# A two-layer transformer kernel: the experts' weight requests reordered, constant matmuls put into five waits, and the mLSTM heads begun right after the copy of their gates

## What is computed

```python
proj = rms_norm(x, norm_mix_g) @ w_in           # dq dk dv | mq mk mv mo | gates
y_da = rms_norm(diff_attention(dq, dk, dv), g)   # 4 heads x 128 columns
y_ml = sigmoid(mo) * normalise(mlstm(mq, mk, mv, gates))
x = x + concat(y_da, y_ml) @ w_out
x = x + cross_attention(rms_norm(x), mem)
# experts: top 2 of 32 for each token, h the normalised rows of an expert
x = x + sum_e weight_e * ((silu(h @ w1[e]) * (h @ w3[e])) @ w2[e])
x4 = rms_norm(rms_norm(x, norm_final_g), ln_a)
b, c, u, z = split(x4 @ w_in_a, 4)              # second block begins
```

## Time and profile before

| | us |
|---|---|
| median of 3 runs | 1514.36 (1511.99 to 1514.66) |
| the profiled execution | 1516.11 |
| its span, first to last instruction | 1514.3 |
| TensorE busy | 1339.1 (88%) |
| VectorE, ScalarE, GpSimd busy | 537.7, 414.4, 392.1 |
| mean granted TensorE clock | 0.946 |

### The profile page before, as it was taken

How to read it: one execution, slowest core, us unless ns; L and a number is a source line. 1 busy time by engine, 2 the same in 40 slices (tenths; PEclk the granted TensorE clock), 3 DMA queues, 4 the chain that set the end, 5 groups by cost and what they waited for, 6 DMA issues and landing times. The chain is left out here.

```text
span 1514.3 us, 16638 instructions
## 1 busy us (share of the span) xinstructions
PE 1339.1 (88%) x6268; PEld 887.8 (59%) x6268; DVE 537.7 (36%) x1074; ACT 414.4 (27%) x809; POOL 392.1 (26%) x372
## 2 busy tenths in 40 slices
PE   7999998999989679988887887883999999999799
PEld 6776775798758533323222222232888887788467
DVE  3649747421052421111111111117241414554753
ACT  5333365154231100000000000005322123444641
POOL 7553233168320112111111111100243550000331
PEclk9999997999999679999999999996999999999999
DMA  7221221144303849999999999994223231232000
GB/s 206 88 81 56 66 102 45 67 167 139 111 5 144 345 190 406 420 423 421 423 422 423 423 422 423 422 381 164 84 84 108 87 104 65 94 100 84 29 22 35
DMA packets 72368, 298.27 MB, mean 197 GB/s; under 512 B 10168, under 2 KB 10216, under 8 KB 51568
## 3 DMA queue, kind: packets, MB, share of 16 engines
q1 hardware_dynamic: 64848, 282.80, 47.6%
q0 software_dynamic: 7456, 14.59, 3.0%
HBM read 293.16 MB, written 12.58 MB: 202 GB/s over the span
## 5 line engine op out<-in xcount | busy, mean ns | idle before, releaser
L740 POOL TENSOR_TENSOR ring_rounded<-ring,ring_rounded 128x512 fp32r<-128x512 f32 x192 | 254.2, 1361 | 328.0 <-ACT ring_rounded L1435 328.0
L862 PE MATMUL bank<-HT_rounded,ring_rounded 128*128 128x512 f32 (+1 forms) x576 | 222.1, 386 | 5.9 <-DVE ring_rounded L2301 4.5
L864 PE MATMUL bank<-HT_rounded,ring_rounded 128*128 128x512 f32 (+1 forms) x576 | 218.7, 380 | 0.0
L863 PE MATMUL bank<-ring_rounded 128*128 128x512 f32 (+1 forms) x576 | 218.5, 379 | 0.0
L1155 PE MATMUL bank<-ring,B 128*64 128x512 f32 x704 | 181.7, 670 | 41.2 <-DMA ring<-in_w 40.3
L1155 PEld LDWEIGHTS bank<-ring,B 128*64 128x64 f32 x704 | 55.7, 152 | 150.9 <-issue 114.6
L2193 DVE TENSOR_TENSOR B<-bank,small 128x512 f32<-128x512 f32 x32 | 22.1, 691 | 331.3 <-PE bank L1145 331.3
L864 PE MATMUL bank<-ring_rounded 128*128 128x512 f32 x352 | 138.2, 393 | 0.0
L1435 ACT ACTIVATE ring_rounded<-ring 128x2048 fp32r<-128x2048 f32 x54 | 102.6, 1915 | 109.4 <-DMA ring<-in_w_in_a 47.5
L862 PEld LDWEIGHTS bank<-HT_rounded,ring_rounded 128*128 128x128 f32 x576 | 109.5, 190 | 33.0 <-issue 9.4
L863 PEld LDWEIGHTS bank<-ring_rounded 128*128 128x128 f32 x576 | 109.5, 190 | 20.4 <-issue 1.0
(11 more groups left out here) (377 smaller groups left out, 1963.7 us busy)
## 6 DMA issues: line engine op xcount, KB each, us to landing
ring<-in_w SPq DMA_DIRECT2D x88, 1024.0 KB, 30.3
A<-in_w SPq DMA_DIRECT2D x21, 2048.0 KB, 28.7
ring<-in_w SPq DMA_DIRECT2D x11, 2048.0 KB, 28.8
XN<-in_w SPq DMA_DIRECT2D x20, 1024.0 KB, 29.1
HT<-in_w SPq DMA_DIRECT2D x20, 1024.0 KB, 32.3
ring<-in_w_in_a SPq DMA_DIRECT2D x16, 1024.0 KB, 5.0
ring<-in_w_in SPq DMA_DIRECT2D x14, 1024.0 KB, 7.1
ring<-in_w_in_b SPq DMA_DIRECT2D x8, 1024.0 KB, 5.3
```

Source lines behind the costliest of these rows:

```text
L740: last = pool.tensor_tensor(r32(lo), lo, r32_read(quarter(g, True)[:, k, :]), ALU.subtract)
L862: pe.matmul(o, r32(a_hi), r32(b_hi), start=first, stop=False)
L863: pe.matmul(o, r32(a_hi), r32(b_lo), start=False, stop=False)
L864: return pe.matmul(o, r32(a_lo), r32(b_hi), start=False, stop=last)
```

## The change

1. `load_expert` takes the pieces to ask for. Experts 3 and 4 are asked for as pieces 0 to 3 of both, then w2 of both.
2. `spin(o, n)` issues n matmuls of the identity with 256 constant columns into a bank that is overwritten next: 5 before `chosen_ready`, 12 before `onehots_ready`, 8 before the first expert, 9 behind `x3_ready` 1 in front of `x4n_ready` 1, 4 before `c0`. In the last expert's step, `down` of expert 30 goes ahead of `hidden` of expert 31.
3. VectorE copies the gates first. The root and the attention heads' normalisation move into the loop (heads 0, 1 after scores 0; heads 2, 3 after rows 0), their transposes to iterations 2 and 3, their splitting behind them, `wo1`'s splitting on ScalarE to iterations 1 and 2. `wo` waits for `y_t` 3's reading.

```diff
@@ first_plan
+        if h == 3:
+            plan += [(("y_t", m), "dve") for m in (2, 3)]
         if h >= 1:
             plan += [(("mh", h - 1, qb), "dve") for qb in range(NT)]
-    plan += [(("y_t", m), "dve") for m in range(8)]
+        if h == 2:
+            plan += [(("y_t", m), "dve") for m in (0, 1)]
+    plan += [(("y_t", m), "dve") for m in range(4, 8)]
@@ SyncE
-            def load_expert(e, slot):
+            def load_expert(e, slot, which=range(5)):
...
+                pieces = list(expert_pieces(e, slot))
+                for n in which:
+                    dst, src, loaded = pieces[n]
                     sp.wait_ge((half_done, half_done, h_done, h_done, y_done)[n], e - 2)
                     sp.dma_start(dst, src).then_inc(loaded, 16)
...
-            load_expert(3, 0)
-            load_expert(4, 1)
+            for which in (range(4), range(4, 5)):
+                load_expert(3, 0, which)
+                load_expert(4, 1, which)
@@ TensorE
+            def spin(o, n):
+
+                for _ in range(n):
+                    pe.matmul(o[:, 0:2 * P], ident, cst[:, 0:2 * P], start=True, stop=True)
...
+                if h == 3:
+                    turn_y(2)
+                    turn_y(3)
                 if h >= 1:
                     for qb in range(NT):
...
+                if h == 2:
+                    turn_y(0)
+                    turn_y(1)
...
-            for m in range(4):
-                turn_y(m)
             outs = [[fill(U, "wo", 0, t)[:, :] for t in range(NT)]]
-            pe.wait_ge(sem("y_low_ready"), 4)
+            wait_emptied(pe, U["y_t", 3])
...
             o = fill(U, "rank")
+            spin(o, 5)
             pe.wait_ge(sem("chosen_ready"), 1)
...
             o = fill(U, "table")
+            spin(o, 12)
             pe.wait_ge(sem("onehots_ready"), 1)
...
+            spin(bank[0], 8)
             step_turn(0, 0)
...
-            for n in range(2, 8):
+            for n in range(2, 7):
                 step(4, n)
+            step_down(4, 6)
+            step(4, 7)
             step_down(4, 7)
...
-                pe.wait_ge(sem("x4n_ready"), t + 1)
                 for b in range(2):
                     o = fill(V, "x4_t", t, b)
+                    if t == 0 and b == 0:
+                        pe.wait_ge(sem("x3_ready"), 1)
+                        spin(o, 9)
+                    pe.wait_ge(sem("x4n_ready"), t + 1)
...
             part = chunk("c0")
+            spin(outs[0], 4)
@@ ScalarE
-            high_parts("wo1")
-            roots(32, 48)
+            def high_y(m):
+
+                o = filled(U["y_t", m])
+                act.activation(r32(yT[:, m, :]), o[:, :], ACT.Copy, scale=g_sub_s).then_inc(sem("high_ready"), 1)
...
+                if h == 0:
+                    roots(32, 48)
+                elif h == 1:
+                    high_half("wo1", 0)
+                elif h == 2:
+                    high_y(0)
+                    high_y(1)
+                    high_half("wo1", 1)
+                else:
+                    high_y(2)
+                    high_y(3)
@@ VectorE
+            o = filled(U["gates_t",])
+            dve.tensor_copy(bmT, o[:, 0:32]).then_inc(done, 1)
             wait_emptied(dve, U["do", 15])
-            rstds(0, [(32, 48, P)])
-            for m in range(4):
+            ms_total[0] += 1
+            dve.tensor_scalar(ms[:, 32:48], ss[:, 32:48], 1.0 / P, EPS, ALU.mult, ALU.add).then_inc(sem("ms_ready"), 1)
+
+            def normalise_o(m):
+
+                if m == 0:
+                    dve.wait_ge(sem("root_ready"), ms_total[0])
+                    own(dve.reciprocal(rstd[:, 32:48], root[:, 32:48]))
...
+            def low_y(m):
+
+                o = filled(U["y_t", m])
+                wait_high()
+                dve.scalar_tensor_tensor(r32(lowT[:, m, :]), o[:, :], g_sub_s, r32_read(yT[:, m, :]), ALU.mult,
+                                         ALU.subtract).then_inc(done, 1)
...
             for h in range(HEADS + 1):
                 if h < HEADS:
                     weighted_scores(h)
+                if h == 0:
+                    normalise_o(0)
+                    normalise_o(1)
+                if h == 3:
+                    low_y(2)
+                    low_y(3)
                 if h >= 1:
                     head_rows(h - 1)
-            for m in range(4):
-                o = filled(U["y_t", m])
-                wait_high()
-                own(dve.scalar_tensor_tensor(r32(lowT[:, m, :]), o[:, :], g_sub_s, r32_read(yT[:, m, :]), ALU.mult,
-                                             ALU.subtract))
...
+                if h == 1:
+                    normalise_o(2)
+                    normalise_o(3)
+                if h == 2:
+                    low_y(0)
+                    low_y(1)
```

More of the change, by code:

```diff
@@ L641, in _ @@
                 sp.dma_start(dst, src).then_inc(loaded, 16)
-            def load_expert(e, slot):
-                for n, (dst, src, loaded) in enumerate(expert_pieces(e, slot)):
+            def load_expert(e, slot, which=range(5)):
+                pieces = list(expert_pieces(e, slot))
+                for n in which:
+                    dst, src, loaded = pieces[n]
                     sp.wait_ge((half_done, half_done, h_done, h_done, y_done)[n], e - 2)
@@ L995, in _, with turn_y @@
             pe.wait_ge(sem("pads_zero"), 2)
+            def turn_y(m):
+                o = fill(U, "y_t", m)
+                pe.wait_ge(sem("y_rows_ready"), m + 1)
+                for t in range(NT):
+                    src = o_rows[:, t, m, :] if m < 4 else hm_rows[:, t, m - 4, :]
+                    last = pe.transpose(o[:, P * t:P * t + P], src, ident)
+                last.then_inc(bank_filled, 1)
             for h in range(HEADS + 1):
@@ L1009, in _ @@
                              lambda k: mv_rows[:, k, h - 1, :], qb + 1)
-            def turn_y(m):
-                o = fill(U, "y_t", m)
-                pe.wait_ge(sem("y_rows_ready"), m + 1)
-                for t in range(NT):
-                    src = o_rows[:, t, m, :] if m < 4 else hm_rows[:, t, m - 4, :]
-                    last = pe.transpose(o[:, P * t:P * t + P], src, ident)
-                last.then_inc(bank_filled, 1)
+                if h == 2:
+                    turn_y(0)
+                    turn_y(1)
             def out_half(outs, n, t, h):
@@ L1043, in _ @@
             last.then_inc(first_half_read, 1)
-            pe.wait_ge(sem("y_low_ready"), 8)
+            pe.wait_ge(sem("y_low_ready"), 4)
             wait_split(pe, chunk_no["wo0"], 1)
@@ L1200, in step @@
                     step_turn(i, n + 1)
-                if not isinstance(e, int) or e > 0:
+                if not isinstance(e, int) or 0 < e < EXPERTS - 1:
                     step_down(i, n - 1)
@@ L1533, in _ @@
                 act.activation(moT[:, m, :], moT[:, m, :], ACT.Sigmoid).then_inc(sem("sig_ready"), 1)
-            for m in range(4):
-                o = filled(U["y_t", m])
-                act.activation(r32(yT[:, m, :]), o[:, :], ACT.Copy, scale=g_sub_s).then_inc(sem("high_ready"), 1)
             roots(48, 64)
@@ L1942, in _ @@
                 dve.tensor_tensor(v, v, r, ALU.mult).then_inc(sem("y_rows_ready"), 1)
-            o = filled(U["gates_t",])
-            dve.tensor_copy(bmT, o[:, 0:32]).then_inc(done, 1)
+            def low_y(m):
[3 more added lines that the diff above has]
+                                         ALU.subtract).then_inc(done, 1)
             dve.wait_ge(sem("em_ready"), 1)
@@ L1986, in _ @@
                     weighted_scores(h)
+                if h == 0:
[4 more added lines that the diff above has]
+                    low_y(3)
                 if h >= 1:
                     head_rows(h - 1)
-            for m in range(4):
-                o = filled(U["y_t", m])
-                wait_high()
-                own(dve.scalar_tensor_tensor(r32(lowT[:, m, :]), o[:, :], g_sub_s, r32_read(yT[:, m, :]), ALU.mult,
-                                             ALU.subtract))
-                dve.nop().then_inc(done, 1)
-                dve.nop().then_inc(sem("y_low_ready"), 1)
+                if h == 1:
[4 more added lines that the diff above has]
+                    low_y(1)
             own(dve.tensor_scalar(ss[:, 48:64], mv[:, 1:32:2], float(P), None, ALU.mult))
```

## The result

| | before | changed |
|---|---|---|
| median, us (executions) | 1514.51 (4) | 1496.61 (4; 1495.49 to 1498.63) |
| ratio, 95% interval | | 0.9882 (0.9859 to 0.9904) |
| the profiled execution | 1516.11 | 1498.63 |
| its span | 1514.3 | 1496.8 |
| mean granted clock | 0.946 | 0.957 |

What follows compares the result with a forecast made beforehand. The weight stream paces the experts' stage; elsewhere TensorE's waits and 1.2 GHz stretches count. Terms 7.1 + 4.2 + 1.0 + 3.0 + 0.9 = 16.2 off the profiled 1516.1 give 1499.9, median 1498.2; range 1492 to 1508.

Steps and rivals of the forecast that it cites:

- heads: Attention heads' stage: head 0's mask begins 9.3 us earlier, first projection matmul sooner; 7.1 us gained.
- ranks, table, first expert: Constant matmuls in the waits before these three raise the clock: 0.8 + 1.8 + 1.6, 4.2 us, between 0 and 5.4.
- I take half of the 3.5 us: Heads: TensorE at 1.2 GHz ends `mh` 0 at 239.9, VectorE asks at 236.3; half this lateness counted, giving 7.1 us.
- I carry the 7.1 us whole to the experts: Behind the heads: the full gain reaches the experts' stage, since nothing between waits for a DMA.
- The Exp table's reload lies beside VectorE's normalising: Heads, ScalarE: reloading the Exp table after the root overlaps VectorE's work; only 1.8 us counted for root, its load and hand-overs.
- Twelve before the table: Twelve constant matmuls in the 8.30 us wait before the table take 11.1 us low, 5.8 high; table gains 1.8.
- Half of the hole is only moved: Weight stream at experts 3 and 4: it still waits for the second `down`, 576.3 to 581.0; 3.0 us gained.
- Last expert: `down` 30 put ahead fills the last `hidden`'s waits; last `down` at 1019.3 instead of 1020.17, 0.9 us gained.
- Rival 1: Constant groups: the clock doesn't rise, overruns of 6.3 us instead of a 5.2 gain, time 1509.7; chance 0.13.
- Rival 2: Heads: TensorE becomes the bound at 1.2 GHz, 42.5 us; gain 2.4 instead of 7.1, time 1502.9; chance 0.15.
- Rival 3: Heads run in lockstep, VectorE waiting at every step; first projection matmul up to 287.8, kernel up to 1525; chance 0.04.
- signs of being wrong: VectorE idle over 1.5 us inside heads; constants ending behind their semaphore; or the stream's start moving without its end.

Runs made afterwards that it cites:

- second comparison: The unmodified changed kernel measured again on another chip (the second profile, "again"): 1500.67 us, ratio 0.9897 against the kernel before.
- constants in two more waits: Changed kernel with 14 constant matmuls ahead of the table, and three each ahead of the first and last expert's turned rows: 1494.16 us, ratio 0.9859.
- early Exp table: Changed kernel plus a one-column Exp on ScalarE right behind the heads' root, to load the table early: 1497.60 us, ratio 0.9887.
- constants ahead of the projection alone: Kernel before with only eight constant matmuls in the 7 us wait ahead of the first projection matmul: 1511.18 us, ratio 0.9963.
- Requests alone: Kernel before with only the new order of requests for experts 3 and 4: 1512.80 us, ratio 0.9982.
- constants alone: Kernel before with only the five groups of constant matmuls, `down` 30 left in its place: 1511.80 us, ratio 0.9974.
- thirty ahead of the table: Changed kernel with 30 constant matmuls ahead of the table instead of 12: 1500.36 us, ratio 0.9899.
- the last kernel: Changed kernel with early Exp table, w2 of experts 3 to 6 behind next pieces, extra expert constants, 16 ahead of table, three ahead of heads: 1486.90 us, ratio 0.9810.

## Why the prediction was right, point by point

**The sum.** 16.2 us predicted, 17.9 measured, 1498.2 against 1496.6; the second comparison measured 15.4. Each part alone has the sign it was given. That the total is so near is partly luck, since the terms miss it both ways: in the second profile by +4.0, +1.6 and +0.1 against -1.8 and -1.7. The sizes, by the table of stretches:

| term | predicted | first profile | again |
|---|---|---|---|
| heads | 7.1 | 8.4 + 1.8 = 10.2 | 9.6 + 1.5 = 11.1 |
| ranks, table, first expert | 4.2 | 1.1 + 2.6 + 1.8 | 1.1 - 0.5 + 1.8 |
| second `hidden` lower | 0 | -1.7 | -1.7 |
| requests and last expert | 3.9 | 5.2 | 5.5 |
| `c0` and behind it | 1.0 | -0.8 | +1.1 |

The row of requests is the stretch from `hidden` 1 to the last `down`, 3.45 and 3.78 shorter, with the 1.7 put back.

**Heads: right mechanism, two steps mis-sized.** "I take half of the 3.5 us" for TensorE's lateness was a mean of two cases, and executions have one or the other, or lie between. Where `m_row` took 1.10, the distance to the first projection matmul was 34.1 to 36.6 (six profiles); where it took 2.05, 37.4 to 39.9 (four). A gain of 5.3 at worst and 8.8 at best was said; 5.3 (39.7 in the kernel with constants in two more waits) and 9.6 were the ends among kernels without the early table. And "I carry the 7.1 us whole to the experts" left out that the projection behind it gains too: the wait of 6.98 us was followed by a low clock from 264.8 to 271.6, and without it 1.3 to 1.9 us came on top. The constants ahead of the projection alone brought 1.5 of these.

"The Exp table's reload lies beside VectorE's normalising" is the step that was wrong. The load belongs to the instruction that needs it and starts only when that one's wait ends (232.45, behind the mask's end at 232.37): 1.3 us. Against it, the second pair of normalisations took 1.27 each and not 1.75, though GpSimd was subtracting all the while (238.26 to 244.10); the first pair took 0.65 each with GpSimd idle, so the four took 3.8 instead of 4.9. In the kernel before too GpSimd was subtracting during all four (224.94 to 236.57) and not only during the three long ones, so the 1.05 us is not the price of every instruction beside it.

**Constants: the price was right, the cover of the table was not.** One takes 0.44 to 0.46 us at the high clock (0.48 said, from `ms`). "Twelve before the table: ... 5.8 high, in 8.30" was read as cover, while it left 3.3 us open, in which the clock fell in four of five profiles. The predicted 1.8 for the table and 1.6 for the first expert are 2.6 + 1.8 in the one case and -0.5 + 1.8 in the other. The Trainium skill, TensorE: Matmul & The Clock Gate, Part 1, says that the point of the change varies between runs of one kernel; two profiles of the same code with the table at 2.20 and 4.13 agree. The second `hidden` was not looked at: behind its wait of 1.6 us it ran in 7.09 in the kernel before, and takes 8.78 now in all five profiles with twelve ahead of the table.

**Requests.** "Half of the hole is only moved": it was a little more than half that closed. The prediction had the stream wait 4.7 us for the second `down` (576.3 to 581.0). Requests alone show 86 of 422 GB/s for 4 us and 383 in the next 4: 3.2 + 0.4 = 3.6. That is 1.1 us less of a wait, so 4.1, or 4.3 by the stretch, instead of 3.0.

**Last expert.** 0.9 said, 1.1 found at the start of the last `down`. In two profiles that `down` then ran low and took 1.7 longer; what of this reaches `c0` differs (33.46 and 32.55 behind it, against 32.75 before).

**`c0`.** x4's transposes and `c0` ran high as planned (1.16 instead of 1.97), but the distance from the last `down` to `c0` goes by scattered rows and VectorE and moved little: 32.6 and 32.8 against 32.75, 31.3 with constants alone. Behind it 1.1 to 1.2 were gained in constants alone and in the changed kernel again; in the first profile, with low stretches near 1390 and 1410 us that those two lack, 1.0 was lost. These stretches are not the whole of it: the early Exp table's profile has both and gained 0.9. What brings them was not tried.

**The rivals.** Rival 1, the clock doesn't rise, did not come about as a whole: the clock rose in the ranks and in the first expert, and fell between them, at the table, in four of five profiles, which made the way from the table to the first `hidden` up to 0.7 us longer than before, and not 6.3. Rival 2, TensorE as the heads' bound, is real in the executions that start low, at 37.4 to 39.9 us rather than its 42.5. Rival 3 did not come near: with the new heads no first projection matmul is later than before. Two of the signs of being wrong came true and did not turn the result. VectorE had an idle time of over 1.5 us inside the heads, 2.33, against a first mask 9.4 us sooner. And in constants alone and in the changed kernel again the eight ended behind the rows that they cover.

## What to carry to other kernels

Cover a wait of TensorE with constant matmuls to near its end, not to its middle: 12 in a wait of 8.3 us lost the clock again in four of five profiles, 14, 16 and 30 kept it in all four. But not beyond: the 4.35 us that 30 ran over came back in full at the last expert when compared with 14, and only against twelve, whose clock fell, were they made up for. These are single profiles, and the clock of one kernel differs between them. When one wait is filled, look at the next short one behind it, count the low clock behind a wait as part of that wait's price, and compare executions by stretches, since one kernel's lie up to 14 us apart. In an in-order queue of requests, put the ones whose slots come free first ahead of the one that waits longest, and go on until no window of the stream is empty.

## What the hardware showed that was not expected

- A removed wait made the heads depend on the clock. With the old heads three profiles of three kernels took 44.97 us to 0.01 (before, requests alone, constants alone), VectorE setting the pace; with the new order, and no early Exp table, seven profiles took 35.4 to 39.7.
- TensorE's idle time of 2.1 us ahead of the heads is followed by a low stretch in all thirteen profiles that have it, for 3.4 us (then `m_row` is at 2.4 GHz again) or for 10 to 20 us (then it is not). With the wait filled to 0.74 the one profile has none. First the changed kernel, its wait and the window behind it by the columns of the earlier trace rows, then that window of the last kernel:

```profile
219.74 0.63 PE L986 MATMUL bank<-cst,E 128*128 128x128 f32 x4 [2.13 <-DVE E L1955]
...
220.50:223.90 3.40, 3.40 (x21) 3.18 (x20) 0.60 (x1) 1.23 (x6) 0.00 (x0) 0.50 0.87 323
```

```profile
217.60:221.00 3.40, 3.29 (x27) 2.92 (x28) 1.26 (x3) 1.29 (x6) 0.00 (x0) 1.00 1.05 396
```

- The idle time of 1.6 us ahead of the second `hidden` is followed by a low stretch in the five profiles with twelve ahead of the table, and in none of the three where it is filled to 0.21. But after the same 1.6 us the clock did not fall in six others, the kernel before and the one with thirty among them: `hidden` 1 took 7.09 there. The wait is not the whole cause.
- Routing, just ahead of the ranks, runs low for 13 us and more in nearly all profiles (497.0 to 510.6 in the first), with waits of 1 us for VectorE in it. In two (the early Exp table and thirty ahead of the table) it was low for 3.4 us only, though their edits do not touch it, and these reached the ranks some 4.3 us sooner (247.5 and 247.6 behind the first projection matmul instead of 251.7 to 252.3). The windows of the first profile and of the early Exp table's, by the same columns as the earlier trace rows (the second also holds the ranks, from 509.45):

```profile
488.00:512.00 24.00, 21.13 (x98) 18.51 (x96) 9.40 (x33) 4.18 (x8) 3.72 (x7) 0.72 0.78 317
```

```profile
488.00:512.00 24.00, 20.28 (x126) 17.62 (x126) 11.92 (x49) 6.54 (x12) 3.73 (x7) 0.93 0.78 313
```

  Constant matmuls in these waits were not tried; by those two profiles some 4 us is the most that they could bring.
